# A two-layer gated mixer trunk: branch C's attention begins among C's value products, three index units go over two tiles at a time, and the last product's tiles end one by one

## The chip, the cores and the metric

The kernel runs on one NeuronCore of a Trainium2 chip. Five engines run side by side, each through its own list of instructions in the order in which the program gives them: TensorE (PE, matmuls and transposes), VectorE (DVE), ScalarE (ACT), GpSimd (POOL) and SyncE (SP, whose queue starts the loads). They wait for each other through semaphores. The metric is the device time of one execution in microseconds (us).

## The reference

Two layers over x, 512 rows (tokens) of 1024 features, all in fp32. Each layer makes one wide projection of x, runs five branches of four heads of 64 on it, gates and merges them, and closes with a projection, a residual and a layer norm:

```python
pr = split_projection(x @ w_in)
...
o_a = dsa_attention(aq, ak, av, iq, ik, pr['i_w'])      # top 128 keys by an index score
o_b = moba_attention(bq, bk, heads(pr['b_v'], N_HEADS, HEAD_DIM))
...
o_c = rms_norm(diff_attention(cq, ck, cv, lam), diff_norm) * (1.0 - lam_init)
...
o_d = mla_attention(qn, qr, kn, kr, dv)
o_e = memory_attention(heads(pr['e_q'], N_HEADS, HEAD_DIM), mkv[:, :, 0], mkv[:, :, 1])
o = jnp.stack([o_a, o_b, o_c, o_d, o_e], axis=2).reshape(b, t, N_BRANCH, BRANCH_W)
y = o * jax.nn.silu(pr['z'].reshape(b, t, N_BRANCH, BRANCH_W))
u = jnp.einsum('btnc,ncd->btnd', y, w_branch)
g = jax.nn.sigmoid(pr['g'].reshape(b, t, N_BRANCH, d))
out = jnp.sum(g * u, axis=2) @ w_out
return layer_norm(DN_ALPHA * x + out, ln_g, ln_b)
```

Branch C's `diff_attention` takes two softmaxes a head, each over keys of 32, and multiplies their difference (the second times `lam`) with the values. Before the first layer x is normalized once.

## The kernel before, in words

**Split products.** The large products keep fp32's accuracy with three fast passes. Each operand is cut into a head (ACT copies it to a rounded type, L1001) and a rest (the operand minus its head). `product3` (L737 to L739) multiplies head by head, head by rest and rest by head. The rests of the weights are made by POOL (L721), the rests of activations by DVE.

**Groups and units.** A weight matrix, named IX, E, A1, ..., O1 in `ORDER`, is worked off in four units; `("grp", c, u, t)` is unit u of matrix c on row tile t (128 rows), six matmuls of up to 512 columns. For the gate matrices gE0 to gD1 a unit is 128 output columns and has five groups: four of products and one for the branch product with `w_branch`. Each product of tile t collects in bank `product` t. A unit's weights are loaded by SP, copied by ACT (`("split", c, u)`) and finished by POOL; the split of a unit stands behind the last group of the unit three places before it, since there are three buffers. Three of the splits stand in the list `start`. The first matrix's first unit of the second layer is split in the first layer's last product ("ahead").

**One list for all engines.** `plan()` writes one list of steps, `PLAN`. Every engine goes through the same list and does its own part of each step: PE's, ACT's, DVE's and POOL's instructions of a step can lie far apart in time, but on no engine does one step overtake another. `spread` lays the steps of a stage evenly, by width, over a stretch of groups that `PLACES` names.

**Branch C.** Its steps are in `diff_steps`. `("qt", "C", e)` transposes queries and keys of two heads (L907, L915) into banks G2 and G3. `("ev", "C", j, m)` is ACT's: two copies of 32 rows of queries and two of keys of map m of head j into `score_operands`. `("er", ...)` is DVE's: the two rests (L1348, L1350). `("S", "C", 2i + m)` is a score map on PE (L949), its mask and maximum on DVE (L1412), its exponential on ACT (L1114). `("W", i)` is DVE's joining of two maps in three instructions, L1464, L1465 and L1467. `("T", "C", i)` transposes the joined map (L962), and `("V", "C", i)` multiplies it with the values (L977) in bank O. The loop gives every unit i two half steps, `first` and `second`. Between half steps stand the groups of other matrices; DVE's part of a gate unit is L1533.

**Index tiles and memory keys.** Behind IX's last unit DVE turns and splits tile t of the index queries and keys: eight instructions, L1212 to L1218 and L1503 to L1506. `("ixj", t)` transposes them on PE (L877, L882); tile 0 needs bank U alone. The banks U and S hold the memory keys until `("ek",)` has moved them: ACT copies four heads, DVE sets four zero halves (L1324) and does for each head a cast (L1328) and a rest (L1329). Two heads done free U, all four free S.

**The last product and the norm.** Behind O1's last unit DVE adds tile t to the residual (L1540) and takes its statistics (L1226, L1231). `("l1", t)` scales the statistics (DVE) and normalizes (ACT, L1010); `("l2", t)` multiplies with the gain (DVE, L1243) and has POOL add the offset in four pieces (L677). Tile 3 has another form: L1283 and L1295, both on DVE. In the first layer the next one follows: the memory products `("mkv", 0)` and `("mkv", 1)`, and `("xj", t, j)`, the transposes of x.

## Time and profile before

| | |
|---|---|
| time, median of 3 runs | 1382.11 us (1380.39 to 1382.39) |
| the profiled execution: time, span | 1384.15 us, 1382.5 us |
| PE, busy with matmuls | 1328.0 us, 96% |
| weight loads of PE | 1130.7 us, 82% |
| DVE, ACT, POOL busy | 661.8, 653.3, 669.9 us, 48%, 47%, 48% |
| PE's mean granted clock | 0.985 |
| chain that ended last, by engine | PE 79%, DVE 12%, ACT 4% |

The engines' busy times are sums over the span; PE alone is near it. The chain that ended last is followed back from the last instruction, at each step to what released it. An engine's idle time costs something only where PE waits for it, or behind PE's last product.

### The profile page before, as it was taken

The numbers are of one execution on the slowest core, as the hardware profiler recorded it, in microseconds if no ns is written. First come the engines' busy times: TensorE is split into PE (matmuls) and PEld (weight loads), VectorE is DVE, ScalarE is ACT, GpSimd is POOL, SyncE is SP. The second block draws the span as 40 slices with busy tenths as digits, with TensorE's granted clock in tenths as the row PEclk, the third lists the DMA queues.
The fourth block names the chain that finished last, engine by engine and source line by source line (L and its number), as shares of the span: only waits on it lengthen the run. The fifth ranks groups of instructions, "written<-read, shape, count | busy, mean of one in ns | idle before, by whom it ended". The sixth has DMA issues, their size and how long they took to land.

```text
span 1382.5 us, 19021 instructions
## 1 busy us (share of the span) xinstructions
PE 1328.0 (96%) x6872; PEld 1130.7 (82%) x6872; DVE 661.8 (48%) x1609; ACT 653.3 (47%) x1296; POOL 669.9 (48%) x850
## 2 busy tenths in 40 slices
PE   6999999999988999999999999999999899999995
PEld 5888878888877898888888888888888779888884
DVE  4646696433155753213265668753322665432044
ACT  4455345454275664423245543555434665643232
POOL 3543453255563444467464435334446434645764
PEclk9899999999998999999999999999999999999998
DMA  7322242231331143232413223223123213323221
GB/s 258 114 77 62 81 114 58 67 88 47 103 95 37 37 123 107 58 107 77 140 49 106 68 71 106 81 58 85 53 74 111 59 33 86 95 65 100 84 77 61
DMA packets 147052, 116.47 MB, mean 84 GB/s; under 512 B 5520, under 2 KB 131856, under 8 KB 146704
## 3 DMA queue, kind: packets, MB, share of 16 engines
q1 hardware_dynamic: 146816, 114.22, 27.8%
q8 instruction: 55, 0.90, 0.3%
q10 hardware_dynamic: 144, 1.05, 0.2%
q14 instruction: 37, 0.30, 0.1%
HBM read 112.10 MB, written 3.15 MB: 83 GB/s over the span
## 4 chain that ended last, share of the span: by engine, by line
PE 79%; DVE 12%; ACT 4%; issue 2%; POOL 1%; DMA 1%; SPq 0%; POOLq 0%; DVEq 0%; ACTq 0%
PE product L737 19%; PE product L738 18%; PE product L739 18%; PE context L977 5%; PE scores L949 3%; PE transposed L962 3%; PE branch_product L737 2%; PE branch_product L739 2%; PE branch_product L738 2%; DVE index_scores L1389 2%; DVE top_eight L1395 1%; DMA residual<-in_x_dram 1%; ACT score_operands L1001 1%; POOL residual L677 1%; DVE vector_scratch L1214 1%
## 5 line engine op out<-in xcount | busy, mean ns | idle before, releaser
L721 POOL TENSOR_TENSOR weights_rest<-raw_weights,weights_head 128x320 fp32r<-128x320 f32 (+3 forms) x672 | 540.1, 836 | 376.8 <-ACT weights_head L1001 376.8
L737 PE MATMUL product<-weights_head,stationary_head 128*128 128x512 f32 (+3 forms) x768 | 291.4, 379 | 7.8 <-POOL weights_rest L721 7.6
L1001 ACT ACTIVATE weights_head<-raw_weights 128x1280 fp32r<-128x1280 f32 (+4 forms) x178 | 198.3, 1115 | 200.3 <-PE product L739 153.5
L739 PE MATMUL product<-weights_head,stationary_rest 128*128 128x512 f32 (+3 forms) x768 | 285.6, 372 | 0.0
L738 PE MATMUL product<-weights_rest,stationary_head 128*128 128x512 f32 (+3 forms) x768 | 285.4, 372 | 0.0
L737 PE MATMUL product<-stationary_head,weights_head 128*128 128x512 f32 x640 | 263.5, 412 | 0.0
L738 PE MATMUL product<-stationary_rest,weights_head 128*128 128x512 f32 x640 | 252.6, 395 | 0.0
L739 PE MATMUL product<-stationary_head,weights_rest 128*128 128x512 f32 x640 | 252.1, 394 | 0.0
L704 POOL TENSOR_TENSOR merged<-merged,activated 128x256 f32<-128x256 f32 x128 | 93.0, 748 | 291.4 <-DVE activated L1533 291.2
L737 PEld LDWEIGHTS product<-weights_head,stationary_head 128*128 128x128 f32 x768 | 145.7, 190 | 29.8 <-POOL weights_rest L721 8.4
L739 PEld LDWEIGHTS product<-weights_head,stationary_rest 128*128 128x128 f32 x768 | 145.4, 189 | 23.7
L738 PEld LDWEIGHTS product<-weights_rest,stationary_head 128*128 128x128 f32 x768 | 145.9, 190 | 20.2
L1114 ACT ACTIVATE probabilities<-probabilities,negated_maxima 128x256 f32<-128x256 f32 (+3 forms) x160 | 86.3, 540 | 155.4 <-DVE negated_maxima L1412 154.4
L739 PEld LDWEIGHTS product<-stationary_head,weights_rest 128*128 128x128 f32 x640 | 121.5, 190 | 27.5
L737 PEld LDWEIGHTS product<-stationary_head,weights_head 128*128 128x128 f32 x640 | 121.8, 190 | 20.8
L738 PEld LDWEIGHTS product<-stationary_rest,weights_head 128*128 128x128 f32 x640 | 122.1, 191 | 19.3
L1533 DVE SCALAR_TENSOR_TENSOR activated<-activated,branch_product 128x512 f32<-128x512 f32 x64 | 44.0, 687 | 154.5 <-PE branch_product L739 149.6
L1412 DVE CUSTOM_DVE_ANT_0 probabilities<-scores,consts_sb 128x256 f32<-128x256 f32 (+3 forms) x136 | 60.4, 444 | 110.8 <-PE scores L949 110.6
L1175 ACT ACTIVATE activated<-product 128x512 f32<-128x512 f32 x80 | 47.7, 596 | 131.4 <-PE product L739 130.5
L977 PEld LDWEIGHTS context<-values_and_gates,probabilities_T 128*128 128x128 f32 x640 | 89.8, 190 | 9.9 <-issue 1.4
L1001 ACT ACTIVATE probabilities_T<-transposed 128x256 f32<-128x256 f32 (+3 forms) x160 | 67.2, 420 | 55.3 <-PE transposed L962 54.0
L949 PE MATMUL scores<-score_operands 128*128 128x256 f32 (+7 forms) x288 | 77.7, 324 | 10.3 <-DVE score_operands L1350 6.1
(200 smaller groups left out, 1812.5 us busy)
## 6 DMA issues: line engine op xcount, KB each, us to landing
raw_weights<-in_w_in_dram SPq DMA_DIRECT2D x104, 512.0 KB, 3.7
raw_weights<-in_w_in_dram SPq DMA_DIRECT2D x72, 256.0 KB, 2.9
raw_weights<-in_w_branch_dram SPq DMA_DIRECT2D x80, 128.0 KB, 3.7
raw_weights<-in_w_out_dram SPq DMA_DIRECT2D x16, 512.0 KB, 3.6
merged<-in_w_mem_kv_dram SPq DMA_DIRECT2D x8, 512.0 KB, 7.3
raw_weights<-in_w_in_dram SPq DMA_DIRECT2D x8, 416.0 KB, 3.1
raw_weights<-in_w_in_dram SPq DMA_DIRECT2D x8, 296.0 KB, 3.8
residual<-in_x_dram SPq DMA_DIRECT2D x4, 512.0 KB, 11.4
```

The costliest lines, as they stand in the source:

```text
L704: ins = nc.gpsimd.tensor_tensor(m[:, part], m[:, part], TH[:, s, part], ALU.add)
L721: ins = nc.gpsimd.tensor_tensor(WL[:, sw, part], RAW[:, sr, part], WH[:, sw, part].bitcast(F32), ALU.subtract)
L737: nc.tensor.matmul(dst, sh, mh, start=start, stop=False)
L738: nc.tensor.matmul(dst, sh, ml, start=False, stop=False)
L739: return nc.tensor.matmul(dst, sl, mh, start=False, stop=stop)
L949: last = nc.tensor.matmul(S[:, 0:w], lhs, rhs, start=i == 0, stop=i == len(passes) - 1)
L977: last = nc.tensor.matmul(O[:, 0:BW][:, t * HD:(t + 1) * HD], PT[:, i * P:(i + 1) * P], v, start=i == 0, stop=i == w // P - 1)
L1001: return nc.scalar.activation(dst, src, ACT.Copy, scale=scale)
L1114: nc.scalar.activation(p, p, ACT.Exp, bias=NMX[:, m:m + 1], scale=-1.0, accum_out=RS[:, j % 2, 2 * t + u % 2 if b == "C" else t:(2 * t + u ...
L1175: nc.scalar.activation(TH[:, s, :], G[u % 2][:], ACT.Tanh, scale=0.5).then_inc(act_out.sem, act_out.step((c, u)))
L1412: nc.vector.tensor_tensor_reduce(probs(b, u)[:, 0:w], S[:, 0:w], bias, -SCALE[b], -TAKEN, ALU.add, ALU.min, NMX[:, u % 4:u % 4 + 1]).then_ ...
L1533: nc.vector.scalar_tensor_tensor(out=TH[:, s, :], in0=TH[:, s, :], scalar=1.0, in1=U[:], op0=ALU.add, op1=ALU.mult).then_inc(used.sem, not ...
```

## The change

Four things move in the list; the instructions stay the same but for their order and, for C's operands, their banks.

1. C's attention is laid from `("C1", 0, 2)` to `("D0", 3, 1)` instead of from `("gA0", 0, 0)` to `("D0", 3, 2)`. Since C1 collects in G2 and G3, the first transposes go to U and O. `W` stands in `first` instead of `second`. An `ev` or `er` step is now queries or keys of one map (`part`), and each stands in a half step of its own.
2. IX's units 0, 1 and 2 run on tile 0, then on tile 1, then each on tiles 2 and 3. The transposes of x's tiles 2 and 3 and `("ek",)` stand further back. In `start` two splits stand ahead of `("ln0", 3)` and `("mkv", 1)`. x's fourth tile is loaded behind two weight loads, and the split "ahead" is gone.
3. O1's unit 0 runs over all tiles; then units 1 to 3 end tile 0, tile 1, tile 2 and tile 3 one after another.
4. `l1` and `l2` of each tile stand nearer to its end.

```diff
 def diff_steps():
-    out = [[("qt", "C", 0)], [("ev", "C", 0, 0)], [("er", "C", 0, 0), ("ev", "C", 0, 1)], [("er", "C", 0, 1)], []]
-    late = []
+    out = [[("qt", "C", 0)]] + [[] for _ in range(5)]
+    early = {}
+    for j in range(NH):
+        for n in range(4):
+            m, part = divmod(n, 2)
+            at = {0: n - 5, 1: n}.get(j, 2 * (4 * j - 3) + 1 + n)
+            early.setdefault(at, []).append(("ev", "C", j, m, part))
+            early.setdefault(at + 1, []).insert(0, ("er", "C", j, m, part))
+    for n in range(5):
+        out[1 + n] += early.get(n - 5, [])
...
         if 0 <= i - 1 < UNITS:
-            second.insert(0, ("W", i - 1))
...
+            first.append(("W", i - 1))
         if i == 4:
-            third.append(("qt", "C", 1))
-        j, m = divmod(i + 3, 4)
-        if j < NH and m < 2 and i < UNITS:
-            third.append(("ev", "C", j, m))
-            late = [("er", "C", j, m)]
-        out += [first, second + third]
+            second.append(("qt", "C", 1))
+        out += [first + early.get(2 * i, []), second + early.get(2 * i + 1, [])]
...
-    ("C attention", ("gA0", 0, 0), ("D0", 3, 2), 0.0),
+    ("C attention", ("C1", 0, 2), ("D0", 3, 1), 0.0),
...
+        order = [(u, t) for u in range(units(c)) for t in range(parts(c))]
+        if c == "IX":
+            order = [(u, t) for t in range(2) for u in range(3)] + [(u, t) for u in range(3) for t in (2, 3)] + [(3, t) for t in range(NT)]
+        elif c == "O1":
+            order = [(0, t) for t in range(NT)] + [(1, 0), (1, 1), (2, 0), (3, 0), (2, 1), (3, 1)] + [(u, t) for t in (2, 3) for u in range(1, 4)]
+        groups += [(c, u, t) for u, t in order]
...
-    start = [("ln0", 0), ("ln0", 1), ("mkv", 0), ("ln0", 2), ("xj", 0, 0), ("xj", 0, 1), ("ln0", 3), splits[0], ("mkv", 1),
-             ("xj", 1, 0), ("xj", 1, 1), ("ln0", 4), splits[1], splits[2]]
-    extra[at[(ORDER[0], 1, 0)]] += [("xj", 2, 0), ("xj", 2, 1)]
-    extra[at[(ORDER[0], 1, 1)]] += [("xj", 3, 0), ("xj", 3, 1)]
-    extra[at[(ORDER[0], 2, 0)]].append(("ek",))
+    start = [("ln0", 0), ("ln0", 1), ("mkv", 0), ("ln0", 2), ("xj", 0, 0), ("xj", 0, 1), splits[0], splits[1], ("mkv", 1),
+             ("xj", 1, 0), ("xj", 1, 1), ("ln0", 3), splits[2], ("ln0", 4)]
+    extra[at[(ORDER[0], 1, 1)]] += [("xj", 2, 0), ("xj", 2, 1)]
+    extra[at[(ORDER[0], 2, 1)]] += [("xj", 3, 0), ("xj", 3, 1)]
+    extra[at[(ORDER[0], 3, 1)]].append(("ek",))
...
-    extra[at[("O1", 2, 1)]] += [("ahead",) + WEIGHTS[0]]
-    extra[at[("O1", 3, 1)]] += [("l1", 0)]
-    extra[at[("O1", 3, 2)]] += [("l1", 1), ("l2", 0)]
-    extra[at[("O1", 3, 3)]] += [("l1", 2), ("l2", 1), ("l1", 3), ("l2", 2), ("l2", 3)]
+    for t in range(NT - 1):
+        i, j = {0: (("O1", 2, 1), ("O1", 3, 1))}.get(t, (("O1", 1, t + 1), ("O1", 2, t + 1)))
+        extra[at[i]].append(("l1", t))
+        extra[at[j]].append(("l2", t))
+    extra[at[("O1", 3, 3)]] += [("l1", 3), ("l2", 3)]
...
+        def qt_banks(b, e):
+            if b == "E":
+                return ("TP", TP), None
+            if b == "C" and e == 0:
+                return ("U", U), ("O", O)
+            return ("G2", G[2]), ("G3", G[3])
...
+                        if b == "C":
+                            m, part = step[3:]
+                            r = slice(at + 32 * m, at + 32 * m + 32)
+                            slot = 4 * (j % 2) + 2 * m + part
+                            src, other = (qs, slice(64, 96)) if part == 0 else (ks, slice(32, 64))
+                            act.wait_ge(t_done.sem, t_done.at(L, (("q", "k")[part], b, e)))
+                            copy(TL[other, slot, :], src[r, :])
+                            copy(TL[0:32, slot, :], src[r, :]).then_inc(moved.sem, moved.step(step))
+                            continue
```

On DVE, behind IX's last unit in the first layer, this is how the list stands before. The casts and differences on `score_operands` are the memory keys, the first `vector_scratch` row opens index tile 0:

```order
L1324 MEMSET score_operands 64x256 x4
L1328 CAST score_operands<-score_operands 64x256
L1329 TENSOR_TENSOR score_operands<-branch_product,score_operands 64x256
...
L1329 TENSOR_TENSOR score_operands<-scores,score_operands 64x256
L1212 TENSOR_TENSOR vector_scratch<-staged_features,consts_sb 128x9x4
```

And of the change, where the last `merged` row closes index tile 1 and the last `vector_scratch` row opens tile 2:

```order
L1216 TENSOR_TENSOR vector_scratch<-staged_features,consts_sb 128x9x4
...
L1508 TENSOR_TENSOR merged<-staged_features,merged 128x32
L1328 MEMSET score_operands 64x256 x4
L1332 CAST score_operands<-score_operands 64x256
L1333 TENSOR_TENSOR score_operands<-branch_product,score_operands 64x256
...
L1333 TENSOR_TENSOR score_operands<-scores,score_operands 64x256
L1216 TENSOR_TENSOR vector_scratch<-staged_features,consts_sb 128x9x4
```

The memory keys stood ahead of all four index tiles; now two tiles stand ahead of them.

On DVE in C's attention of the first layer, around the join of head 0's last but one unit (the rows on `map_factors` and the one behind them), before:

```order
L1412 ISA index_scores,negated_maxima<-scores,consts_sb 128x512
L1412 ISA negated_maxima 128x1
L1533 SCALAR_TENSOR_TENSOR activated<-activated,branch_product 128x512
L1464 RECIPROCAL map_factors<-row_sums 128x1
L1465 SCALAR_TENSOR_TENSOR map_factors<-map_factors,lambdas,row_sums 128x1
L1467 SCALAR_TENSOR_TENSOR probabilities<-probabilities,map_factors 128x384
L1412 ISA index_scores,negated_maxima<-scores,consts_sb 128x512
```

And of the change:

```order
L1414 ISA index_scores,negated_maxima<-scores,consts_sb 128x512
L1414 ISA negated_maxima 128x1
L1466 RECIPROCAL map_factors<-row_sums 128x1
L1467 SCALAR_TENSOR_TENSOR map_factors<-map_factors,lambdas,row_sums 128x1
L1469 SCALAR_TENSOR_TENSOR probabilities<-probabilities,map_factors 128x384
L1535 SCALAR_TENSOR_TENSOR activated<-activated,branch_product 128x512
L1414 ISA index_scores,negated_maxima<-scores,consts_sb 128x512
```

The gate's operation, which waits for PE's branch product, stood ahead of the join and stands behind it now.

On DVE at the end of the last layer, from tile 2's residual on, before:

```order
L1540 SCALAR_TENSOR_TENSOR residual<-product2,residual 128x512
L1226 BN_STATS half_tile_stats<-residual 128x6
...
L1243 TENSOR_TENSOR residual<-residual,values_and_gates 128x1024
L1540 SCALAR_TENSOR_TENSOR residual<-product3,residual 128x512
L1226 BN_STATS half_tile_stats<-residual 128x6
...
L1243 TENSOR_TENSOR residual<-residual,values_and_gates 128x1024
L1283 SCALAR_TENSOR_TENSOR residual<-residual,norm_stats,values_and_gates 128x1024
L1243 TENSOR_TENSOR residual<-residual,values_and_gates 128x1024
```

And of the change:

```order
L1247 TENSOR_TENSOR residual<-residual,values_and_gates 128x1024
L1542 SCALAR_TENSOR_TENSOR residual<-product2,residual 128x512
L1230 BN_STATS half_tile_stats<-residual 128x6
...
L1247 TENSOR_TENSOR residual<-residual,values_and_gates 128x1024
L1542 SCALAR_TENSOR_TENSOR residual<-product3,residual 128x512
L1230 BN_STATS half_tile_stats<-residual 128x6
L1235 BN_AGGR norm_stats<-half_tile_stats 128x2
L1287 SCALAR_TENSOR_TENSOR residual<-residual,norm_stats,values_and_gates 128x1024
```

Each gain (L1243, L1247) stood one or two tiles' residuals behind its own; now tile 2's stands ahead of tile 3's residual, and none behind.

## Rows read from the trace of the kernel before

**Rows 1.** Who waited for whom, PE: us in total, times, longest us.

```profile
PE transposed L962 <- DVE probabilities L1467: 8.8, 10, 1.8
...
PE product L737 <- POOL weights_rest L721: 7.6, 3, 4.1
...
PE scores L949 <- DVE score_operands L1350: 6.1, 4, 1.5
```

**Rows 2.** Stretches: from:to, us, busy PE, PEld, DVE, ACT, POOL, PEclk, DMA, GB/s.

```profile
385.00:460.00 75.00, 66.94 (x315) 54.54 (x314) 44.67 (x112) 48.19 (x102) 33.75 (x43) 0.93 0.20 59
...
415.00:445.00 30.00, 26.56 (x118) 21.95 (x119) 17.77 (x47) 15.77 (x37) 11.32 (x14) 0.85 0.14 43
...
1057.00:1132.00 75.00, 66.90 (x318) 54.40 (x317) 44.77 (x112) 48.48 (x103) 34.80 (x44) 0.95 0.20 58
...
1090.00:1120.00 30.00, 27.07 (x130) 22.40 (x129) 16.86 (x44) 15.95 (x36) 9.82 (x12) 0.89 0.14 43
...
1343.50:1365.40 21.90, 21.90 (x97) 17.83 (x95) 7.51 (x17) 6.13 (x8) 5.64 (x8) 1.00 0.00 0
...
1365.40:1382.50 17.10, 0.02 (x1) 0.00 (x0) 9.12 (x12) 2.03 (x3) 12.12 (x12) 0.62 0.31 123
```

**Rows 3.** Timeline, C's attention: start us, us, engine, line, out<-in [idle before <-releaser].

```profile
407.66 2.42 ACT L1001 ACTIVATE score_operands<-product 32x512 fp32r<-32x512 f32 x4
...
410.73 0.69 DVE L1533 SCALAR_TENSOR_TENSOR activated<-activated,branch_product 128x512 f32<-128x512 f32 x1 [1.67 <-ACT activated L1175]
...
412.27 1.05 DVE L1467 SCALAR_TENSOR_TENSOR probabilities<-probabilities,map_factors 128x384 f32<-128x384 f32 x1
...
413.46 0.52 PE L962 MATMUL transposed<-consts_sb,probabilities 128*128 128x128 f32 x3 [1.78 <-DVE probabilities L1467]
```

**Rows 4.** Timeline, the end of C0's last rotation.

```profile
365.09 0.97 DVE L1218 TENSOR_TENSOR staged_features<-vector_scratch 128x128 f32<-128x128 f32 x1
```

**Rows 5.** Timeline, memory keys and index tiles on DVE, first index transpose on PE.

```profile
44.82 1.41 DVE L1324 MEMSET score_operands<- 64x256 f32 x4
...
49.46 0.43 DVE L1329 TENSOR_TENSOR score_operands<-branch_product,score_operands 64x256 fp32r<-64x256 f32 x1
...
51.78 0.51 DVE L1212 TENSOR_TENSOR vector_scratch<-staged_features,consts_sb 128x36 f32<-128x36 f32 x1
...
56.88 0.73 DVE L1212 TENSOR_TENSOR vector_scratch<-staged_features,consts_sb 128x36 f32<-128x36 f32 x1
...
57.24 0.27 PE L882 MATMUL branch_product<-consts_sb,merged 128*96 128x128 f32 x1
...
59.53 0.20 DVE L1212 TENSOR_TENSOR vector_scratch<-staged_features,consts_sb 128x36 f32<-128x36 f32 x1
```

**Rows 6.** Timeline, the start.

```profile
26.01 1.28 DVE L1226 BATCH_NORM_STATS2 half_tile_stats<-residual 128x6 f32<-128x512 f32 x2
...
32.96 0.68 DVE L1308 TENSOR_TENSOR stationary_rest<-context,stationary_head 128x512 fp32r<-128x512 f32 x1
...
33.06 0.61 PE L737 MATMUL product<-weights_head,stationary_head 128*128 128x296 f32 x1 [4.12 <-POOL weights_rest L721]
```

**Rows 7.** Timeline, PE at the layer boundary.

```profile
711.78 0.40 PE L737 MATMUL product<-weights_head,stationary_head 128*128 128x296 f32 x1 [2.26 <-POOL weights_rest L721]
```

**Rows 8.** Timeline, the last product's end.

```profile
1350.33 2.82 POOL L721 TENSOR_TENSOR weights_rest<-raw_weights,weights_head 128x320 fp32r<-128x320 f32 x4 [2.62 <-ACT weights_head L1001]
...
1357.29 0.69 DVE L1540 SCALAR_TENSOR_TENSOR residual<-product,residual 128x512 f32<-128x512 f32 x1 [12.18 <-PE product L739]
...
1365.84 12.12 POOL L677 TENSOR_TENSOR residual<-residual,values_and_gates 128x256 f32<-128x256 f32 x12 [12.68 <-DVE residual L1243]
...
1368.99 1.74 DVE L1283 SCALAR_TENSOR_TENSOR residual<-residual,norm_stats,values_and_gates 128x1024 f32<-128x1024 f32 x1
...
1372.51 2.15 DVE L1295 SCALAR_TENSOR_TENSOR residual<-residual,norm_stats,values_and_gates 128x512 f32<-128x512 f32 x2
...
1378.37 1.26 SPq L664 DMA_DIRECT2D out_dram<-residual  x2
```

More of the change, by code:

```diff
@@ L131, in diff_steps @@
             first.append(("S", "C", 2 * i))
[L132 removed]
+            second.insert(0, ("S", "C", 2 * i + 1))
         if 0 <= i - 1 < UNITS:
[L134 to L146 removed]
+            first.append(("W", i - 1))
+        if i == 4:
+            second.append(("qt", "C", 1))
+        out += [first + early.get(2 * i, []), second + early.get(2 * i + 1, [])]
     return out
@@ L208, in plan @@
     for c in ORDER:
-        pairs = {"IX": (0,), "O1": (2,)}.get(c, ())
-        for u in range(units(c)):
-            if u in pairs:
-                groups += [(c, u + i, t) for t in range(NT) for i in range(2)]
-            elif u - 1 not in pairs:
-                groups += [(c, u, t) for t in range(parts(c))]
+        order = [(u, t) for u in range(units(c)) for t in range(parts(c))]
[4 more added lines that the diff above has]
+        groups += [(c, u, t) for u, t in order]
     at = {g: i for i, g in enumerate(groups)}
@@ L592, in _ @@
                 for i, item in enumerate(LOADS):
+                    if L == 0 and i == 2:
+                        load_x(3)
                     if L == 0 and i == NRAW:
@@ L712, in _ @@
                                                 ALU.mult).then_inc(normed.sem, normed.step(("zn", t)))
-                    if step[0] in ("split", "ahead"):
-                        item, L2 = step[1:], L + (step[0] == "ahead")
-                        if L2 == DEPTH or L > 0 and step == ("split",) + WEIGHTS[0]:
-                            continue
+                    if step[0] == "split":
+                        item = step[1:]
                         pool.wait_ge(head.sem, head.at(L, step))
-                        sw, sr, n = w_slot(L2, item), raw_slot(item), size(item[0])
+                        sw, sr, n = w_slot(L, item), raw_slot(item), size(item[0])
                         for at in range(0, n, PIECE):
@@ L902, in _ @@
                             pe.wait_ge(roped.sem, roped.at(L, (b + "0", NT - 1)))
-                        name, bank = ("TP", TP) if b == "E" else ("G2", G[2])
+                        (name, bank), second = qt_banks(b, e)
                         claim(name)
@@ L1022, in _ @@
                     kind = step[0]
-                    if kind in ("split", "ahead"):
-                        item, L2 = step[1:], L + (kind == "ahead")
-                        if L2 == DEPTH or L > 0 and step == ("split",) + WEIGHTS[0]:
-                            continue
+                    if kind == "split":
+                        item = step[1:]
                         rw = raw[raw_slot(item)]
-                        act.wait_ge(rw.sem, rw.at(L2, item))
-                        unread(act, L2, item)
+                        act.wait_ge(rw.sem, rw.at(L, item))
+                        unread(act, L, item)
                         n = size(item[0])
-                        copy(WH[:, w_slot(L2, item), 0:n], RAW[:, raw_slot(item), 0:n]).then_inc(head.sem, head.step(step))
+                        copy(WH[:, w_slot(L, item), 0:n], RAW[:, raw_slot(item), 0:n]).then_inc(head.sem, head.step(step))
                     elif kind == "ln0" and L == 0 and step[1] < NT:
```

62 lines of the change are left out of this document (22 added, 40 removed).

## The prediction

> **What bounds the kernel now.** I read three views in this order. The list of who waited for whom says which idle times PE (TensorE) has [rows 1]: its transposes wait 8.8 us for VectorE's (DVE's) joined maps of branch C (L1467), its products 7.6 us for GpSimd's (POOL's) weight rests (L721), its scores 6.1 us for C's operand rests (L1350). The table of stretches gives them places [rows 2]. In the last product, 1343.5 to 1365.4, PE is busy throughout: where nothing waits, an order can win nothing. In C's attention, 385 to 460, it is busy 66.94 of 75 us, so 8.1 us idle, and 66.90 in the second layer, 8.1 again. After such idle times the granted clock falls to the lower level, 1.2 GHz: a stretch at mean clock c loses up to busy x (1 - c), which is 26.56 x 0.15 = 4.0 us from 415 to 445 and 27.07 x 0.11 = 3.0 in layer 1. C's stage costs 16.2 + 7.0 = 23.2 us. The last 17.1 us hold no product. The timeline then shows how each wait comes about. The profiled execution took 1384.15 us (span 1382.5), the median is 1382.11; the sum is made on the profile, and 2.0 us come off.
>
> **C's attention.** DVE joins two maps in three instructions, the last at 412.27; they stand behind the gate product L1533 (410.73), and PE's transposes, due 1.78 us earlier, begin at 413.46 [rows 3]. ScalarE (ACT) copies a head half's queries and keys in one piece of four, 2.42 us, in front of the next exponentials. The change (1) puts the join a half step earlier, ahead of L1533, and so gives a late one a whole half step more; (2) cuts the four copies and two rests into pieces of two (1.2 us) and one (0.69), one a half step; (3) starts 14 groups earlier. A group of six 128x512 matmuls is 1.36 us (16 of them fill the 21.9 us of the last product [rows 2]), so C's stage has some 89 us of products instead of 71, for 44 steps instead of 43: 2.0 us a half step instead of 1.65. No instruction is added. The densest places stay, where the operands of heads 1, 2 and 3 are prepared: ACT then has 2.4 us of copies in a full step, beside two exponentials and a weight copy. I leave one wait of nearly 0.6 us at each of three places a layer, a third of the 1.78, which is 3.4 us, and 0.8 of slow clock. Gain 23.2 - 4.2 = 19.0; bounds 23.2 if all goes, 0 if the waits only move.
>
> The earlier start needs C's rotations finished when PE comes to its transposes, now behind C1's third group. C1's 16 groups end where C's stage begins, at 385.1, so the third ends 13 x 1.36 = 17.7 us before, at 367.4; the last rotation ends at 365.09 + 0.97 = 366.1 [rows 4]. Cover 1.3 us, cost nothing; without it, that much a layer. The banks U and O, which hold the first transposes now, are claimed again at gA0's branch product and at the first context, three groups or more behind the last rest that reads them: nothing.
>
> **The memory keys.** This speaks against the change. The step ("ek",) goes from behind index unit 2's first tile to behind unit 3's second: on DVE from ahead of index tile 0 to behind tile 1. PE's first index transpose claims bank U, which is free when two of ek's four heads are done. Now the memsets (44.82) and the heads are done while DVE would wait, tile 0 begins at 51.78, tile 2 at 59.53, and PE does the transpose at 57.24, without a wait [rows 5]. Then: tiles 0 and 1 until 59.53, memsets 1.41, four operations of 0.43 with their gaps 1.75: U is free at 62.7, and PE waits 62.7 - 57.2 = 5.5 us. The second layer has the same steps: 5.5 again. Bounds: tile 0 takes 5.1 us here, tile 1, from 56.88 on, 2.65; two of the shorter make the wait 3.1, two of the longer 8. Behind it the clock falls: two idle times of 1.8 and 1.5 us in 411 to 416 were followed by most of the 4.0 us above. I take 2.5 a layer, between 0 and the whole 4.0. Loss: 2 x (5.5 + 2.5) = 16.0.
>
> Tile 0 is slow and tile 1 is not because POOL's subtractions run beside the first: both have the same eight instructions. The Trainium skill, "SBUF — State Buffer", "Who interferes with whom", says that a VectorE instruction with both inputs in SBUF contends with a GpSimd instruction that reads SBUF, and that the later one blocks for the whole of the other. By that rule the two head operations that read a PSUM bank keep their 0.43 in any case, and a move of the tiles under POOL's splits would take the wait to its upper bound of 8, the sum to -1.5. The trace agrees in one place: the operation at 49.46 takes 0.43 us with the splits under way.
>
> **The start.** Two splits come ahead of the fourth row tile's norm, the third behind it. Now the norm's statistics begin at 26.01 and PE's first index product at 33.06, after 4.12 us of idling: a chain of 7.05 us, statistics, scale, norm, split, rest [rows 6]. Then: units 0 and 1 are split early, and PE's first two groups run from 28.9, at full clock, until 30.5. But the statistics stand behind tile 1's rests. These end 0.7 us behind its last copy now (32.96 + 0.68); the copies, two of 0.6, follow PE's 28.9: 30.5. Unit 2 is ready at 30.5 + 7.05 = 37.6. PE idles 7.1 us and stands at 37.6 where it stood before at 37.7. What differs is the clock, which has then still to recover: 0 to 2 us, half of the 4.0 above, since before it was slow here too; I take 1.0. The load of x's fourth tile goes behind two weight loads; it is asked for 4.5 us later than before: nothing.
>
> **The layer boundary.** Unit 1's split stands ahead of the second memory product now, and the 2.26 us wait at 711.78 goes [rows 7]. Unit 2's stays behind tile 1's copies, ready when unit 1's was, at 711.7; PE comes to it after two groups of 0.82 from 708.5, at 710.1: a wait of 1.6, gain 0.7. The split that was done ahead of the layer runs between the two memory products: nothing, since POOL's adds are done by then.
>
> **The last product.** Unit 3 follows three groups (4.1 us) behind unit 0's end instead of eight. POOL has its rests at 1350.33 + 2.82 = 1353.15 [rows 8]; PE would be there at 1343.5 + 7 x 1.36 = 1353.0, less than 0.3 with the signal: +0.6 for two layers. In return tiles 0, 1 and 2 are done 10.9, 8.2 and 4.1 us before PE's end. A tile takes DVE 1.7 us (0.69, 0.73 and 0.2). Tile 0's gain ends at -5.2, tile 1's, behind ACT's norm, at -1.6, tile 2's at 3.3; POOL's twelve adds, 12.12 us, end at about 7.5 instead of 12.6, and DVE goes on with tile 3, 1.7, 1.74 and 2.15 us, until 9.1. The last two stores, issued at 1378.37 or 13.0 behind PE's end, then are issued from 8.9 on: the end is 12.7 behind PE's instead of 17.1. Gain 4.4; 2 if POOL's adds slow every DVE instruction, 7 if none.
>
> **Sum:** -19.0 - 4.4 - 0.7 + 0.6 + 1.0 + 16.0 = -6.5. 1384.15 - 6.5 = 1377.6 in a profile, 1382.1 - 6.5 = 1375.6 as the median. Most of what C's stage gives is spent at the index transposes.
>
> **Rivals.** (a) The wait behind ek is short, because POOL's splits fall between DVE's tiles and the clock holds. For it: 3.1 is its lower bound, and tile 1's 2.65 us show what DVE does undisturbed. Against it: POOL's splits stay near where they are. With 3.1 and no slow clock the sum is -16.3: 1365.8. Chance 0.2. (b) The other side: ACT and DVE bind C's stage in its dense places. For it: they are busy 48.19 and 44.67 of 75 us, no work goes, and a dense full step of ACT, 2.4 + two exponentials and their reads + weight copy, comes to some 5.6 us against PE's 4.9. Against it: the joins' 8.8 us are taken off L1533 outright. If 10.7 us of the 23.2 stay, nothing is gained; at half, 11.6, the time is 1383.0. Chance 0.15. (c) The new idle times of 5.5 and 7.1 us are longer than C's and cost the clock's whole price, 4.0 a layer and 2 at the start, 4.0 more than I took: 1379.6. Chance 0.15. The Trainium skill, "TensorE: Matmul & The Clock Gate", "Part 1: The HAM clock gate", says that the gate follows how busy the array has been, which is this case; the trace agrees, with 0.85 granted behind C's idle times. (d) All as in the sum, 1371 to 1379: 0.5.
>
> **How the numbers follow.** The range, 1366 to 1381.5, takes in (a) but its deepest part, (c), and the milder half of (b); the likeliest case's own is 1371 to 1379. About 0.2%, 2.8 us, is what a measurement of this kernel tells from no change. Faster by more, below 1379.3: (a), most of (d), a third of (c): 0.74. Within: the rest of (c) and of (d), some of (b): 0.14. Slower: 0.12.
>
> **What would show it.** PE's wait for the joined maps near zero and C's stage busy above 97%; a new line in the list of waits, PE's index transpose for DVE's score operands, twice, some 5 us each, with the clock falling behind it; one wait of 7 us at 30 us; a tail of 12 to 13 us. I am wrong if the new line is missing or under 3 us, or if C's stage still shows waits above 1 us.

## The result, and the profile of the changed kernel

The changed kernel takes 1388.82 us (median of 4 executions, 1388.65 to 1389.16) against 1381.25 us (median of 4, 1379.29 to 1382.39): a ratio of 1.0057, 95% interval 1.0039 to 1.0074. It is slower by 7.6 us, where 6.5 us less were forecast. Its profiled execution took 1388.78 us, with a span of 1387.1 us against 1382.5. One execution of experiment 9 ran at a granted clock of 0.75 (1630.56 us) and is left out of its median.

Who waited for whom on PE in the changed kernel, as in [rows 1]:

```profile
PE branch_product L887 <- DVE score_operands L1333: 11.7, 2, 5.9
PE product L742 <- POOL weights_rest L726: 10.4, 2, 8.9
PE scores L955 <- DVE negated_maxima L1414: 8.3, 8, 2.1
PE scores L955 <- DVE score_operands L1353: 6.9, 4, 2.0
...
PE product L742 <- DVE stationary_rest L1312: 1.4, 2, 0.7
```

The 8.8 us for joined maps are gone without a rest. In their place stands a new first line, the index transposes for the memory keys' operands, twice 5.9 us. Three lines grew: the weight rests from 7.6 to 10.4 us, the masks' maxima from 3.9 to 8.3, the operand rests from 6.1 to 6.9.

The stretches that answer to [rows 2], C's attention in both layers, the last product and the tail behind it:

```profile
385.00:465.00 80.00, 73.81 (x361) 60.84 (x360) 48.70 (x121) 52.61 (x113) 41.86 (x53) 0.98 0.25 70
1057.00:1140.00 83.00, 76.96 (x376) 63.48 (x375) 49.62 (x122) 55.78 (x117) 44.15 (x55) 0.98 0.26 72
1353.60:1375.60 22.00, 21.92 (x96) 17.46 (x94) 9.49 (x18) 6.70 (x8) 10.99 (x15) 1.00 0.03 11
1375.60:1387.10 11.50, 0.00 (x0) 0.00 (x0) 6.72 (x10) 1.53 (x2) 5.04 (x6) 0.66 0.40 161
```

PE idles 6.2 of 80 us and 6.0 of 83 in C's stage: a little less than the 8.1 before, and far from none. The tail is 11.5 us instead of 17.1.

Timeline at the memory keys (answers to [rows 5]): DVE's index tiles 0 and 1, the memsets, the second of the four heads' rests, and PE.

```profile
55.07 0.64 DVE L1216 TENSOR_TENSOR vector_scratch<-staged_features,consts_sb 128x36 f32<-128x36 f32 x1 [6.04 <-ACT staged_features L1007]
...
60.30 0.73 DVE L1216 TENSOR_TENSOR vector_scratch<-staged_features,consts_sb 128x36 f32<-128x36 f32 x1
...
63.66 1.41 DVE L1328 MEMSET score_operands<- 64x256 f32 x4
...
66.19 0.43 DVE L1333 TENSOR_TENSOR score_operands<-branch_product,score_operands 64x256 fp32r<-64x256 f32 x1
66.77 0.42 PE L887 MATMUL branch_product<-consts_sb,merged 128*96 128x128 f32 x1 [5.87 <-DVE score_operands L1333]
```

Tile 0 takes 5.2 us, tile 1 3.4, and the memsets and two heads 3.0; DVE idled 6.0 us ahead of all of it, longer than these 3.0.

Timeline at C's attention (answers to [rows 3]): the two kinds of wait that it has now.

```profile
401.87 0.97 DVE L1519 SCALAR_TENSOR_TENSOR values_and_gates<-activated,product 128x256 f32<-128x256 f32 x2 [1.06 <-ACT values_and_gates L1007]
402.76 0.42 DVE L1414 CUSTOM_DVE_ANT_0 index_scores<-scores,consts_sb 128x256 f32<-128x256 f32 x1
...
403.24 0.44 PE L955 MATMUL scores<-score_operands 96*128 96x384 f32 x1 [2.08 <-DVE negated_maxima L1414]
...
435.82 0.69 DVE L1414 CUSTOM_DVE_ANT_0 index_scores<-scores,consts_sb 128x512 f32<-128x512 f32 x1
...
436.55 0.69 DVE L1353 TENSOR_TENSOR score_operands<-product,score_operands 32x512 fp32r<-32x512 f32 x1
...
437.38 0.30 PE L955 MATMUL scores<-score_operands 96*128 96x128 f32 x1 [1.52 <-DVE score_operands L1353]
...
458.37 0.69 DVE L1535 SCALAR_TENSOR_TENSOR activated<-activated,branch_product 128x512 f32<-128x512 f32 x1 [1.01 <-ACT activated L1179]
...
460.54 0.30 PE L955 MATMUL scores<-score_operands 96*128 96x128 f32 x1 [2.00 <-DVE score_operands L1353]
```

At 403.24 the mask (L1414), which frees the scores' bank, stood on DVE behind C1's gate products (L1519), and these waited 1.06 us for ACT. At 437.38 the last operand rest of a head stood behind the mask of the score just made. The second kind comes back at 460.54 with 2.00 us; there a gate operation (L1535), which waited 1.01 us for ACT, stood ahead of mask and rest. All three come back in the second layer.

Timeline of the start (answers to [rows 6]): statistics of the last row tile, a gain of DVE with POOL idle, the last tile's norm, the third split, DVE's gain and offset beside it, and PE.

```profile
30.41 1.28 DVE L1230 BATCH_NORM_STATS2 half_tile_stats<-residual 128x6 f32<-128x512 f32 x2
...
31.85 1.17 DVE L1247 TENSOR_TENSOR residual<-residual,values_and_gates 128x1024 f32<-128x1024 f32 x1
...
33.87 1.24 ACT L1016 ACTIVATE residual<-residual,norm_stats 128x1024 f32<-128x1024 f32 x1 [1.61 <-DVE norm_stats L1241]
35.02 0.68 ACT L1007 ACTIVATE weights_head<-raw_weights 128x592 fp32r<-128x592 f32 x1
...
35.82 3.54 POOL L726 TENSOR_TENSOR weights_rest<-raw_weights,weights_head 128x320 fp32r<-128x320 f32 x2
...
35.14 1.81 DVE L1247 TENSOR_TENSOR residual<-residual,values_and_gates 128x1024 f32<-128x1024 f32 x1 [1.31 <-ACT residual L1016]
36.98 1.76 DVE L1268 TENSOR_TENSOR residual<-residual,values_and_gates 128x1024 f32<-128x1024 f32 x1
...
39.41 0.62 PE L742 MATMUL product<-weights_head,stationary_head 128*128 128x296 f32 x1 [8.92 <-POOL weights_rest L726]
...
49.18 0.37 PE L742 MATMUL product<-weights_head,stationary_head 128*128 128x296 f32 x1 [0.69 <-DVE stationary_rest L1312]
```

In the kernel before, the two pieces of the split that stands behind this norm took:

```profile
31.42 1.58 POOL L721 TENSOR_TENSOR weights_rest<-raw_weights,weights_head 128x320 fp32r<-128x320 f32 x2
```

The layer boundary on PE (answers to [rows 7]):

```profile
718.30 0.40 PE L742 MATMUL product<-weights_head,stationary_head 128*128 128x296 f32 x1 [1.45 <-POOL weights_rest L726]
...
722.87 0.66 PE L861 MATMUL transposed<-consts_sb,residual 128*128 128x128 f32 x4 [0.17 <-DVE stationary_rest L1312]
725.63 0.37 PE L742 MATMUL product<-weights_head,stationary_head 128*128 128x296 f32 x1 [0.69 <-DVE stationary_rest L1312]
```

And the end (answers to [rows 8]): the first tile's sum, POOL's last adds, DVE's last steps, the last stores.

```profile
1364.68 0.69 DVE L1542 SCALAR_TENSOR_TENSOR residual<-product,residual 128x512 f32<-128x512 f32 x1 [9.80 <-PE product L744]
...
1378.84 3.75 POOL L684 TENSOR_TENSOR residual<-residual,values_and_gates 128x256 f32<-128x256 f32 x4 [1.95 <-DVE residual L1247]
...
1380.37 1.64 DVE L1287 SCALAR_TENSOR_TENSOR residual<-residual,norm_stats,values_and_gates 128x1024 f32<-128x1024 f32 x1
...
1382.12 1.68 DVE L1299 SCALAR_TENSOR_TENSOR residual<-residual,norm_stats,values_and_gates 128x512 f32<-128x512 f32 x2
...
1383.17 1.08 SPq L671 DMA_DIRECT2D out_dram<-residual  x2
```

**Where the time went.** Both traces hold the same 6872 matmul instructions, so PE's delay against the kernel before can be read along the program, from the ends of the matmuls of the same number, in us:

| stretch | delay that it adds | forecast |
|---|---|---|
| start | +3.5 | +1.0 |
| memory keys, both layers | +8.5, +8.15 | +16.0 |
| C's attention, both layers | -5.8, -5.2 | -19.0 |
| last product's unit 3, both layers | +0.37, +0.37 | +0.6 |
| layer boundary | +0.4 | -0.7 |
| tail behind PE's end | -5.5 | -4.4 |
| sum | +4.8 (spans: +4.6) | -6.5 |

The medians differ by more, 7.6 us: the profiled execution of the kernel before (1384.15 us) lay 2.9 above the median beside the changed kernel (1381.25), and the changed kernel's lay on its own. In which stretch these 2.9 us lie is not known; part of what the table gives C's attention may be theirs.

### The profile page after: what moved, and what is told of

Read it like the earlier page. It is cut to its first block, busy times and chain, and to the rows that moved or that the text cites. A ratio compares the mean times of both kernels' runs of the same rounds, so it can differ in the third digit from the quotient of the medians.

```text
span 1387.1 us, 19021 instructions
## 1 busy us (share of the span) xinstructions
PE 1325.9 (96%) x6872; PEld 1128.8 (81%) x6872; DVE 660.5 (48%) x1609; ACT 653.3 (47%) x1296; POOL 666.0 (48%) x850
## 4 chain that ended last, share of the span: by engine, by line
PE 79%; DVE 13%; ACT 4%; issue 2%; DMA 1%; POOL 1%; SPq 0%; DVEq 0%; ACTq 0%
PE product L742 18%; PE product L744 18%; PE product L743 18%; PE context L983 5%; PE scores L955 3%; PE transposed L968 3%; PE branch_product L742 2%; PE branch_product L744 2%; PE branch_product L743 2%; DVE index_scores L1391 2%; DVE top_eight L1397 1%; PE product L842 1%; DMA merged<-in_w_mem_kv_dram 1%; DVE vector_scratch L1218 1%; DVE vector_scratch L1216 1%
## 5 line engine op out<-in xcount | busy, mean ns | idle before, releaser
L742 PE MATMUL product<-weights_head,stationary_head 128*128 128x512 f32 (+3 forms) x768 | 293.7, 382 | 11.8 <-POOL weights_rest L726 10.4
L1535 DVE SCALAR_TENSOR_TENSOR activated<-activated,branch_product 128x512 f32<-128x512 f32 x64 | 43.9, 686 | 149.6 <-PE branch_product L744 145.4
L1414 DVE CUSTOM_DVE_ANT_0 probabilities<-scores,consts_sb 128x256 f32<-128x256 f32 (+3 forms) x136 | 60.5, 445 | 111.1 <-PE scores L955 110.7
L1179 ACT ACTIVATE activated<-product 128x512 f32<-128x512 f32 x80 | 47.7, 596 | 131.9 <-PE product L744 131.1
```

Source lines behind the costliest of these rows:

```text
L742: nc.tensor.matmul(dst, sh, mh, start=start, stop=False)
L1179: nc.scalar.activation(TH[:, s, :], G[u % 2][:], ACT.Tanh, scale=0.5).then_inc(act_out.sem, act_out.step((c, u)))
L1414: nc.vector.tensor_tensor_reduce(probs(b, u)[:, 0:w], S[:, 0:w], bias, -SCALE[b], -TAKEN, ALU.add, ALU.min, NMX[:, u % 4:u % 4 + 1]).then_ ...
L1535: nc.vector.scalar_tensor_tensor(out=TH[:, s, :], in0=TH[:, s, :], scalar=1.0, in1=U[:], op0=ALU.add, op1=ALU.mult).then_inc(used.sem, not ...
```

## The experiments

Each time is the median of its executions; "before" is the kernel before on the same chip beside it (1381.06 to 1381.94 us).

**1. The memory keys sooner.** The changed kernel with one step moved:

```diff
-    extra[at[(ORDER[0], 3, 1)]].append(("ek",))
+    extra[at[(ORDER[0], 1, 2)]].append(("ek",))
```

> The changed kernel with one step moved: the memory keys ("ek",) behind index group (1, 2), the ninth, where they stood by count before. Theory: PE's two waits of 5.87 and 5.86 us for bank U and the slow clock behind them (8.5 and 8.2 us in the ledger of delays) come from this place alone, so the time falls by 15 to 17 us, to 1372 to 1374. Rival: DVE is short of time there in any case and the wait goes to the index tiles; then the fall is under 8 us and PE waits for rotated tiles instead.

1372.67 us (1372.36 to 1374.53), ratio to before 0.9939 [0.9927, 0.9951]. 16.2 us less than the changed kernel; both 5.9 us waits are gone from the list, 11.7 us, and the remaining 4.5 are the clock behind them: the mean granted clock was 0.66 from 64 to 74 us and from 740 to 750 in the changed kernel, and it is 1.00 from 53 to 66 and from 715 to 745 here. The place of this one step turned a gain into the loss.

**2 to 4. One part at a time.** The kernel before with C's part alone (steps, place, banks, pieces); with the last product's order and tail alone; with the index units' order, start and memory keys alone.

```diff
-    ("C attention", ("gA0", 0, 0), ("D0", 3, 2), 0.0),
+    ("C attention", ("C1", 0, 2), ("D0", 3, 1), 0.0),
...
-            second.insert(0, ("W", i - 1))
+            first.append(("W", i - 1))
```

> The kernel before with C's attention alone as changed (its place, its banks, its pieces, the join's half step). Theory, from the ledger: 5.8 and 5.2 us less in the two layers, so 11 us less than before, 1370 to 1371, with the same three kinds of waits as in the whole change (1.5 and 2.0 us for operand rests, 2.1 us for a mask) and no wait for joined maps. Rival: the gain seen in the ledger hangs on PE being later for other reasons; then it is under 8 us.

1372.83 us (1367.42 to 1373.82), 0.9932 [0.9919, 0.9945]: 9.1 us less than before, half of the 19.0.

```diff
+        if c == "O1":
+            groups += [(c, u, t) for u, t in [(0, t) for t in range(NT)] + [(1, 0), (1, 1), (2, 0), (3, 0), (2, 1), (3, 1)] + [(u, t) for t in (2, 3) for u in range(1, 4)]]
+            continue
...
-    extra[at[("O1", 2, 1)]] += [("ahead",) + WEIGHTS[0]]
```

> The kernel before with the last product's order alone as changed, without the split ahead of the layer. Theory: the tail is 11.5 us instead of 17.1 and PE waits about 0.4 us in each layer for unit 3's rests, sum about -5 us, 1376 to 1377. At the layer boundary the first split now stands where it did in the list, behind the fourth norm's place: up to 2 us of it may go there. Rival: the tail's gain is used up at the boundary and nothing is left.

1376.62 us (1373.12 to 1379.07), 0.9957 [0.9944, 0.9970]: 5.3 us less.

```diff
+        if c == "IX":
+            groups += [(c, u, t) for u, t in [(u, t) for t in range(2) for u in range(3)] + [(u, t) for u in range(3) for t in (2, 3)] + [(3, t) for t in range(NT)]]
+            continue
...
-    extra[at[(ORDER[0], 2, 0)]].append(("ek",))
+    extra[at[(ORDER[0], 3, 1)]].append(("ek",))
```

> The kernel before with the index units' order, the start list, the later transposes of x, the later memory keys and the later load of x's fourth tile as changed. Theory: +3.5 at the start, +8.5 and +8.2 for the memory keys, about 0 at the layer boundary: +20 us, 1401 to 1402. Rival: the parts are not additive, and alone this one costs under 16 or over 24 us.

1405.73 us (1405.24 to 1406.51), 1.0175 [1.0162, 1.0188]: 23.9 us more, where about 20 were expected. Along PE, 12.0 of it come up to the end of layer 0's memory keys, 8.8 at layer 1's, 0.4 at the layer boundary and 1.1 in layer 1's C stage; the rest lies between the profiled executions and the medians.

**5. C's part and the last product's, without the index units' part**: the edits of 2 and 3 together, none of 4.

> The kernel before with C's attention and the last product's order as changed, the index part left as it was. Theory: the two add, -9.1 and -5.3 us as measured alone, so 1367 to 1369, faster than both kernels. Rival: both gains hang on the same idle time or on the clock's phase, then the sum is under 11 us.

1366.31 us (1363.45 to 1368.90), 0.9896 [0.9878, 0.9913]: 14.9 us less, and the parts give 9.1 + 5.3 = 14.4. They add up. This kernel is the base of the next three.

**6. Operands sooner.** The evictions and rests of heads 2 and 3 one half step earlier:

```diff
-            at = {0: n - 5, 1: n}.get(j, 2 * (4 * j - 3) + 1 + n)
+            at = {0: n - 5, 1: n}.get(j, 2 * (4 * j - 3) + n)
```

> As e5, with the copies and rests of the operands of heads 2 and 3 one half step sooner. Theory: the two waits a layer for operand rests (1.5 and 2.0 us, and the slow clock that may follow) come from the last rest standing on DVE behind the mask of the score before it; a half step sooner they go to under 0.5 us, the time falls by 5 to 8 us, to 1360 to 1363. Rival: DVE and ACT are short of time in these steps whatever the order; then the same 1.5 and 2.0 us appear as waits for a mask and the time stays within 2 us of e5.

1360.81 us (1359.24 to 1361.16), 0.9856 [0.9841, 0.9871]: 5.5 us less than its base. Of the waits for operand rests, 1.52 and 2.00 us a layer, one of 0.72 for a mask is left; the wait of 2.09 us for the first mask stays.

**7. The join late.** The join in the second half step, as before, at the new place:

```diff
         if 0 <= i - 1 < UNITS:
-            first.append(("W", i - 1))
+            second.insert(0, ("W", i - 1))
```

> As e5, with the join W back in the second half step. Theory: the join's earlier half step is what took the 8.8 us of waits for joined maps away, so 3 to 8 us of them come back. Rival: the wider stretch did it, a half step being 2.0 us of products instead of 1.65; then the waits stay away and the time is that of e5 within 1.5 us.

1378.46 us (1377.51 to 1381.15), 0.9988 [0.9979, 0.9997]: 12.1 us more than its base, above what was expected. The waits for joined maps come back, longer than before (3.0, 1.5 and 2.9 us a layer). Without the join's earlier half step C's part gains nothing at this place: 1378.46 against the 1376.62 of the last product's part alone.

**8. The old place.** C's steps begin where they did, with the banks of before; pieces and half steps stay new:

```diff
-    ("C attention", ("C1", 0, 2), ("D0", 3, 1), 0.0),
+    ("C attention", ("gA0", 0, 0), ("D0", 3, 2), 0.0),
...
-            if b == "C" and e == 0:
-                return ("U", U), ("O", O)
```

> As e5, with C's attention at its old place (gA0 to D0's fifteenth group) and in its old banks, but in the new pieces and half steps. Theory: the three waits a layer at 389 us for masks behind C1's gates (2.6 us) go, since no gate of C1 is left beside it, but 19 us less of products stand beside the same steps, and the waits for operand rests grow to over 2.5 us each; sum 0 to 8 us slower than e5. Rival: the place gives nothing, the pieces and the join all; then it is faster than e5 by the 5 us of the vanished mask waits.

1356.46 us (1355.57 to 1358.26), 0.9825 [0.9811, 0.9839]: 9.9 us less than its base, twice what the rival gave. My theory, that the wider place is part of the gain, falls. Place and banks moved together, so their shares are not parted. The list of waits of this kernel, and PE's first wait at a mask:

```profile
PE product L742 <- POOL weights_rest L726: 7.3, 3, 3.1
PE scores L955 <- DVE negated_maxima L1414: 6.1, 8, 1.5
...
PE scores L955 <- DVE score_operands L1353: 2.5, 2, 1.2
...
403.44 0.44 PE L955 MATMUL scores<-score_operands 96*128 96x384 f32 x1 [0.58 <-DVE negated_maxima L1414]
```

**9. The old place, operands sooner.** Both edits.

> The kernel with C's new pieces and the new end of the last product, C's attention at the place and with the banks of before, and the operands of heads 2 and 3 made one half step sooner. Theory: a wait for operand rests that stands behind a mask on DVE is made by the half step at which the rest is queued, at either place. At the old place 1.24 us a layer of it are left; sooner by a half step they go, or leave some 0.5 us behind: 1 to 2.5 us faster than the kernel at the old place (1356.46 us), so 1354 to 1355.5. Rival: the sooner evictions lie on ACT ahead of the probabilities that the old place needs at once, and a wait for a mask or a probability grows by as much: 1356 to 1358.

1356.36 us (1355.11 to 1357.22), 0.9821 [0.9807, 0.9834]: no difference from the old place alone. It is the rival's result. There is no trace of these executions, so what took the place of the 1.24 us wait is not shown.

**10. The old place, the join late.** Of C's part only the new pieces are left, beside the last product's part.

> C's attention at the place of before, new pieces, and the maps joined in the second half step again, as before. Theory: the half step of the join is what removed before's waits for joined maps (8.8 us in all) and carries most of the C part's gain; with it put back the kernel stands 8 to 13 us above the one at the old place (1356.46 us): 1364 to 1369, and 8 to 12 under the kernel that has the last product's part alone (1376.62 us), if the pieces are worth that. Rival A: the pieces alone do nothing: then 1374 to 1377. Rival B: the join costs little at the old place, where gates give the other engines time: 1357 to 1360.

1367.67 us (1367.33 to 1368.34), 0.9907 [0.9892, 0.9922]: 11.2 us more than with the join early (experiment 8; the kernels before beside the two, 1381.24 and 1381.06, agree), and 8.95 less than the kernel with the last product's part alone (1376.62, taken on another chip). So at the old place the pieces give 7 to 9 us (7 by the two ratios to before; the other kernel's executions lie 6 us apart) and the join 11. Less the 9.9 that the new place costs, that is the 10.3 us between experiments 3 and 5 by arithmetic; measured on the kernel before, C's part alone gave 9.1.

PE across the two stretches of C's attention, 383 to 480 and 1050 to 1147, in the base, with the join late, at the old place, and there with the join late, the columns as in [rows 2]:

```profile
383.00:480.00 97.00, 91.17 (x467) 78.19 (x466) 55.39 (x145) 55.13 (x122) 46.02 (x59) 0.96 0.20 54
1050.00:1147.00 97.00, 90.97 (x461) 77.53 (x461) 56.77 (x149) 56.80 (x125) 47.85 (x62) 0.96 0.20 54
```

```profile
383.00:480.00 97.00, 87.81 (x444) 74.40 (x443) 57.71 (x145) 54.48 (x121) 45.73 (x57) 0.96 0.20 54
```

```profile
383.00:480.00 97.00, 94.21 (x505) 81.71 (x504) 58.30 (x159) 64.74 (x144) 48.41 (x62) 1.00 0.21 57
1050.00:1147.00 97.00, 94.16 (x510) 82.11 (x509) 61.28 (x175) 64.58 (x151) 45.00 (x58) 1.00 0.22 58
```

```profile
383.00:480.00 97.00, 91.87 (x478) 78.83 (x477) 58.71 (x152) 62.06 (x133) 44.90 (x58) 0.98 0.21 56
```

At the old place PE idles 2.8 of 97 us, at full clock; at the new one 5.8 and 6.0, at 0.96; with the join late 9.2. To part waits from clock I summed, from each trace, PE's 1800th to 2500th matmul (from about 360 to 500 us, layer 0): the time between the two, PE's idle time in it, and the rest, which is the same work and so measures the clock.

| kernel | time | idle | rest |
|---|---|---|---|
| before | 142.9 | 8.1 | 134.8 |
| changed | 137.1 | 6.2 | 130.9 |
| C's part alone | 135.5 | 6.2 | 129.3 |
| 5, base | 138.7 | 6.2 | 132.5 |
| 6, operands sooner | 134.6 | 3.4 | 131.2 |
| 7, join late | 142.7 | 9.6 | 133.1 |
| 8, old place | 132.1 | 2.9 | 129.2 |
| 10, old place, join late | 137.1 | 5.2 | 131.9 |

The least rest, 129.2, is the work at full clock. The kernel before lost 8.1 us to waits and 5.6 to the clock in this stretch, the changed one 6.2 and 1.7. In layer 1, from the 5236th matmul to the 5936th, idle and rest are 8.2 and 133.1 before, 6.0 and 130.0 in the changed kernel, with 128.4 the least of all. Each row is one execution.

**11. The third split ahead of the last tile's norm**, added to the first experiment's kernel:

```diff
-    start = [..., splits[0], splits[1], ("mkv", 1),
-             ("xj", 1, 0), ("xj", 1, 1), ("ln0", 3), splits[2], ("ln0", 4)]
+    start = [..., splits[0], splits[1], splits[2], ("mkv", 1),
+             ("xj", 1, 0), ("xj", 1, 1), ("ln0", 3), ("ln0", 4)]
```

> The changed kernel with the memory keys six groups sooner, as in the first run, and the split of the third index unit's weights ahead of the last tile's norm on ACT and on POOL. Theory: the changed start costs 3.5 us because TensorE waits 8.92 us for that split, which stands behind the norm and whose two pieces take 3.54 us beside DVE's two-input operations. Ahead of the norm they take 1.6 us and end near 30.5; TensorE then runs its six groups of the first two tiles and waits for x tile 3 instead, until some 37.5 us, 9 us sooner than the 46.4 at which the changed kernel takes that tile: 5 to 9 us faster than the first run (1372.67 us), so 1364 to 1368. Rival: the last tile's norm and TensorE's transposes of the second tile are themselves pushed back by the split on ACT, or the tile's arrival decides: within 2 us of 1372.67.

1363.24 us (1362.20 to 1363.97), 0.9873 [0.9859, 0.9886]: 9.4 us less than the first experiment's 1372.67 (on another chip, its before within 0.9 us), a little more than expected. By the two traces 6.8 us come by PE's 200th matmul, in the index units; 1.7 come at the layer boundary, where the same list orders layer 1, and 1.6 in layer 1's C stage, where the waits are the same and the clock is not. The timeline of its start, the six pieces of three splits and PE's wait:

```profile
24.77 4.67 POOL L726 TENSOR_TENSOR weights_rest<-raw_weights,weights_head 128x320 fp32r<-128x320 f32 x6 [0.87 <-ACT weights_head L1007]
...
35.72 0.63 PE L861 MATMUL transposed<-consts_sb,residual 128*128 128x128 f32 x4 [3.05 <-POOL residual L684]
```

Each piece takes 0.78 us now, the rests are ready at 29.4 and the 8.92 us wait is gone. PE runs on into the second tile and waits 3.05 us for the norm's offset instead.

**12. Together.** The whole change, with the keys sooner, the third split ahead, and C at the old place.

> The whole change with three of its places mended: the memory keys six groups sooner, the third split ahead of the last tile's norm, and C's attention at the place and with the banks of before. Theory: the three effects lie in different stretches and add up. The second run that moved C's attention back was 9.9 us faster than its partner (1366.31 to 1356.46); from 1363.24 us that gives 1353.4, within 1351 to 1356. Rival: with the index units in their new order the clock or a wait at C's start stands otherwise and less than half of it comes: 1358 to 1363.

1355.64 us (1354.81 to 1356.94), 0.9810 [0.9797, 0.9823]: 26.3 us less than before and 33.2 less than the change as made. The step back to the old place gave 7.6 us here, not 9.9, and the time is at the upper end of what was expected. Its list of waits begins:

```profile
PE scores L953 <- DVE negated_maxima L1412: 6.1, 8, 1.5
...
PE transposed L859 <- POOL residual L682: 3.0, 1, 3.0
PE scores L953 <- DVE score_operands L1351: 2.5, 2, 1.2
```

It is the fastest kernel of the study, but only 0.8 us from the one of experiment 8, which leaves the index units as they were: the ranges of the two overlap, and the reordering of the index units, even mended, isn't shown to give anything there.

## Why the prediction was wrong

**The step that failed** is C's gain: "one wait of nearly 0.6 us at each of three places a layer" and 0.8 of slow clock, so 23.2 - 4.2 = 19.0. The trace shows 5.8 + 5.2 = 11.0, and C's part alone gave 9.1. What failed is the idle time: it fell by 4.0 us in both layers (16.2 to 6.2 + 6.0) where I took 12.8 (16.2 - 3.4). The other 7.0 are the clock, where I took 6.2; there I had priced the kernel before too low, 4.0 us in layer 0 where the table above gives 5.6, so that the clock's part came out near by luck. Three places there are, but of 2.08, 1.52 and 2.00 us a layer. I had priced them as remnants of the old wait for the join, at 0.6. They are other waits: a mask behind C1's gate products, and operand rests behind masks. Both follow from the edits themselves. The rests are queued in the half step in which the mask is, one half step before use; and the place reaches back into C1, whose gate products need DVE and ACT. Experiments 6 and 8 show each: moved half a step, the rests' waits go (5.5 us); at the old place, with its banks, the first wait falls from 2.08 to 0.58, the second from 1.52 to 0.75 and the third from 2.00 to 1.24.

**The argument for the place** was wrong in kind. "Some 89 us of products instead of 71" counted PE's time for each half step, and not what else the other engines have to do in the added stretch. With its banks it cost 9.9 us (experiment 8). I had no rival with this sign for the place by itself; rival (b), that ACT and DVE bind in dense places, came near it in its amount (half of the gain stays: 1383.0) and was given 0.15.

**The join** was right in mechanism: the waits for joined maps, 8.8 us, are gone. Its half step is worth 12.1 us at the new place and 11.2 at the old, clock included. The pieces, worth 7 to 9 us at the old place, had no term of their own in the sum.

**The memory keys** were right: 5.87 us instead of 5.5, and 2.5 a layer for the clock as taken; 16.6 us instead of 16.0. Experiment 1 gave 16.2 back. Tile 0 took 5.2 us (5.1 before) and tile 1 3.4 instead of 2.65.

**The start** cost 3.5 instead of 1.0. The chain of 7.05 us from statistics to the rest was carried over from [rows 6], where the rest's two pieces took 1.58 us. Behind the last norm they meet DVE's gain (L1247) and offset (L1268) and take 3.54, so the chain is 9.0 and the wait 8.92. The Trainium skill, "SBUF — State Buffer", "Who interferes with whom", says that such an operation and POOL's hold a common port one after the other; the trace agrees, DVE's L1247 taking 1.81 us beside POOL's operations and 1.17 at 31.85 with POOL idle. I had used that rule at the memory keys and not here. The 0.69 us wait for x tile 3's rest, which I did not list, is in it too.

**The layer boundary** cost 0.4 instead of giving 0.7: the wait of 1.6 us that I computed is there as 1.45, but x tile 3's transposes stand closer to its products, 0.69 + 0.17 us. That makes 2.31 us of waits against the 2.26 of before; for the other 0.3 the trace shows no wait.

**The last product** was right, 0.37 us a layer for unit 3, and the tail a little better than I took: 11.5 us behind PE's end instead of 12.7, so -5.5 against -4.4; alone it gave 5.3. **Rival (c)**, the clock's whole price, did not come: 2.6 and 2.3 us behind the two waits at the keys, not 4.0. Against the sum, C's attention lacks 8.0 us, the start 2.5, the boundary 1.1 and the keys 0.65, the last product gave 1.0 more, and 2.9 are the profiled execution of the kernel before, on which the sum was made; together they are the 14.1 us between -6.5 and +7.6.

## What to carry to other kernels

When a step is moved from one slot of a static order to another, list what stands ahead of it on every in-order engine at the new slot, with its waits, and not only the time that the bottleneck engine gives there: a longer stretch beside a busier neighbour is no more room. A wait is gone for good only if the new order puts no other operand work behind the instruction that the bottleneck waits for at each step, or else the wait comes back under another name. And where a setup step's bank is claimed by a later stage, moving the step later moves that claim onto the path; one line of a plan was worth 16 us here.

## What the runs showed of the hardware

**The clock behind a wait of two microseconds is no fixed price.** C's part alone ran six times: 1367.42 us once, with full clock through C's stage in that execution's trace (rest 129.3 us), though its waits are the changed kernel's, 2.09, 1.51 and 2.00 us; the other five executions, of which there is no trace, took 1372.81 to 1373.82, at a mean granted clock of 0.988 or 0.989 over the whole, against 0.992. Its stretch in layer 1, against the changed kernel's:

```profile
1057.00:1142.00 85.00, 81.60 (x437) 71.03 (x436) 49.72 (x129) 47.88 (x105) 41.09 (x52) 1.00 0.20 53
```

```profile
1057.00:1142.00 85.00, 78.96 (x384) 65.12 (x383) 49.92 (x124) 56.20 (x119) 44.15 (x55) 0.98 0.27 75
```

The base of experiment 5, too, takes 1363.45 and 1364.66 us at a clock of 0.995 and 1366.31 to 1368.90 at 0.990 or 0.991. An estimate from these clocks: 0.003 to 0.004 of 1366 us is 4 to 5.5 us, most of the 5.4 to 6.4 between the executions of C's part alone. In which stretch the five ran slower is not shown. The Trainium skill, "TensorE: Matmul & The Clock Gate", "Part 1: The HAM clock gate", says that the number of slow matmuls differs between runs of one kernel; these runs don't contradict it, with 5.4 us between two executions. For a sum, such waits want two prices and a range.

**POOL's subtractions and DVE's two-input operations** of 1024 columns lengthen each other at the start: a piece of 0.78 us takes 1.73 to 1.84, the gain of 1.17 us takes 1.81. DVE's L1268 begins at 36.98 and ends at 38.74, some 1.1 us behind POOL's first piece, which started at 35.82 and took up to 1.84; that is about what DVE's gain takes alone: the times fit one waiting for the other's end, which is argued from these rows.
